# Two up tiles at a time by seven block products, and the norm's row scale at the end of the ConvFFN

## The chip, the cores and the metric

One Trainium2 chip, one of its cores. The metric is the device time in microseconds from launch to end. The engines are TensorE (matmuls into PSUM), VectorE, ScalarE, GpSimd and SyncE; each runs its own queue in order and waits on semaphores. SyncE and GpSimd issue nearly all DMAs here. In the profile they are PE, DVE, ACT, POOL and SP.

## The reference

One inference step of a decoder trunk: 512 prompt rows and 8 sample rows, 520 columns here since activations are kept with features on partitions. D_MODEL = 1024, two layers. Layer 0 mixes by a short gated convolution, layer 1 by dilated attention in three groups; each is followed by a ConvFFN with D_FF = 2816:

```
def rmsnorm(x, g):
    r = lax.rsqrt(jnp.mean(xf * xf, axis=-1, keepdims=True) + EPS)
    return (xf * r).astype(x.dtype) * g

def convffn(h, hist, w_gate, w_up, conv_w, conv_b, w_down):
    gconv, new_hist = causal_dwconv(h @ w_gate, hist, conv_w)     # 3 taps along the sequence
    return (jax.nn.silu(gconv + conv_b) * (h @ w_up)) @ w_down, new_hist

hp = rmsnorm(xp, norm_ffn[i])
fp, fh_p = convffn(hp, ...)
xp = xp + fp
```

Everything is float32. The last rows of h @ w_gate are outputs too.

## The kernel before

**Products.** A float32 operand is split in two parts for the float32r matmul: a high part (a rounding copy, ScalarE) and a low part (operand less high part, VectorE). Of a product the terms high x high, high x low and low x high are made. The weights stream from HBM in chunks of 1024 rows x 128 columns (512 KB) into four slots `wraw`; ScalarE makes `wh`, VectorE `wl`, two buffers each. A chunk is prepared when the chunk two before it has been used (`step` and `splits`). SyncE loads the chunk four ahead when a slot's low part is made (`load`, L464).

**A chunk on TensorE** (`wide_products`, L2016 to L2020) is eight k-steps. Each has five matmuls: one of 512 columns that streams high and low part of half the activations beside each other, and four of 256 or 264. `products` (L1998) makes the same in six matmuls. The three terms stream 3 x 520 = 1560 columns a k-step in both.

**ConvFFN.** Gate and up: 22 tiles of 128 features in 11 bodies of four chunks (gate, up, gate, up), into the PSUM banks `acc[:, 0]` and `acc[:, 1]`. In layer 1 the first body's second pair goes to `M` and `N`, since it begins while the attention's output is still being added. The norm's weight is on the activations ahead of the product; its row scale r is known only a chunk or more after the stage has begun, so it is applied at the read-outs: `wide_gate_out` multiplies a gate by r (ScalarE first copies the low x wide part, `keep_low`), then come the convolution (`conv_act` on ScalarE, `taps` on VectorE), silu (L1028), silu x r (`gate_rows`, L1572), and the product with the up tile (`product_out`), whose high and low part (`y_hi`, `y_lo`) are made at once. Down: eight tiles, each from three chunks that cover the 22 k-steps, then `residual` adds the tile to x.

**Entering a stage.** `rms` on ScalarE copies the high part of the square sum, takes what work is due (`early`), then waits for TensorE's mean square and makes r with Ln and Exp; the table for silu is loaded after it. `rms` on VectorE makes the low part of the square sum, does its own early split and waits for r.

**Order.** All orders are written out by hand, engine by engine. The bodies are hardware loops (`Fori`) on each engine, with semaphore targets worked out in registers. GpSimd copies the KV caches from HBM to HBM in pieces that wait for counts of used chunks.

## Time and profile before

| | |
|---|---|
| runs | 1195.51, 1195.6, 1196.05 us; median 1195.6 us |
| profiled execution | span 1194.2 us from first to last instruction |
| granted TensorE clock, mean | 1.000 |
| instructions | 26318, of these 10352 matmuls |
| VectorE, ScalarE busy | 774.9 us, 546.5 us |
| DMA | 193.19 MB, 162 GB/s mean |

The page gives no time of the profiled execution outside its span; its span is 1.4 us under the median of the runs. Times below are microseconds from the span's start. In an order of time a row is one instruction, or several merged (x2), with start and duration; listed durations of neighbours overlap on an engine, so the pace is the distance of the starts. Gate/up of layer 0 runs from about 186 to 420 us, that of layer 1 from about 834 to 1072.

### The profile page before, as it was taken

The page shows a single profiled execution, that of the slowest core. Times are in us where ns is not written, and L with a number is a line of the kernel's source. Part 1 is how long each engine was busy: PE and PEld are TensorE (multiplying, and loading weights), DVE is VectorE, ACT ScalarE, POOL GpSimd, SP SyncE. Part 2 cuts the span into 40 slices and gives each one's busy share as a digit, 9 for nine tenths or more (in the row PEclk, how much of TensorE's full clock was granted, in tenths as well). Part 3 has the DMA queues.
Part 4 walks back from the last instruction along what each step waited for, and adds up shares of the span by engine and source line. Part 5 has one row for each costly group of instructions (what it writes and reads, how often), then busy time and mean ns, then how long its engine had stood idle before and what let it go on. Part 6 is the DMA issues. An engine that isn't in the chain of part 4 may idle for free.

```text
span 1194.2 us, 26318 instructions
## 1 busy us (share of the span) xinstructions
PE 1188.3 (100%) x10352; PEld 1139.5 (95%) x10352; DVE 774.9 (65%) x1425; ACT 546.5 (46%) x956; POOL 21.1 (2%) x50
## 2 busy tenths in 40 slices
PE   9999999999999999999999999999999999999999
PEld 8999999999999999999999999988999999999998
DVE  6766677766777644445686776868887776774333
ACT  6333345444444532225466565556654454442221
POOL 0000000000000000000000000000000000000000
PEclk9999999999999999999999999999999999999999
DMA  8454535565454555455567766669545454546542
GB/s 222 127 164 150 177 110 172 172 191 160 145 152 136 169 159 155 143 174 170 157 204 195 221 176 192 194 159 238 151 147 153 137 173 154 151 146 183 133 115 44
DMA packets 285909, 193.19 MB, mean 162 GB/s; under 512 B 40433, under 2 KB 282153, under 8 KB 284678
## 3 DMA queue, kind: packets, MB, share of 16 engines
q1 hardware_dynamic: 282636, 137.04, 42.2%
q0 software_dynamic: 1792, 54.43, 12.8%
q8 instruction: 57, 0.93, 0.4%
q10 hardware_dynamic: 1402, 0.61, 0.2%
q14 instruction: 22, 0.18, 0.0%
HBM read 184.52 MB, written 64.16 MB: 208 GB/s over the span
## 4 chain that ended last, share of the span: by engine, by line
PE 93%; DVE 4%; ACT 1%; DMA 1%; issue 1%; SPq 0%; DVEq 0%; POOL 0%; ACTq 0%; POOLq 0%
PE acc L2016 22%; PE acc L1998 15%; PE acc L2020 12%; PE acc L2017 11%; PE acc L2018 11%; PE acc L2019 11%; PE acc L2054 3%; PE N L1985 1%; PE M L2054 1%; PE N L2309 1%; DVE wl L1294 1%; PE acc L2289 1%; PE M L1985 1%; DVE u L1795 1%; PE M L2258 1%
## 5 line engine op out<-in xcount | busy, mean ns | idle before, releaser
L886 ACT ACTIVATE wh<-wraw 128x1024 fp32r<-128x1024 f32 (+1 forms) x211 | 218.0, 1033 | 276.4 <-PE acc L2020 176.4
L1294 DVE TENSOR_TENSOR wl<-wraw,wh 128x1024 fp32r<-128x1024 f32 (+1 forms) x211 | 252.8, 1198 | 130.3 <-ACT wh L886 102.5
L2016 PE MATMUL acc<-h_both,wh 128*128 128x512 f32 x832 | 315.6, 379 | 0.0
L2020 PE MATMUL acc<-h_both,wl 128*128 128x264 f32 x832 | 231.3, 278 | 0.0
L2017 PE MATMUL acc<-h_both,wh 128*128 128x264 f32 x832 | 229.6, 276 | 0.0
L2018 PE MATMUL acc<-h_both,wh 128*128 128x264 f32 x832 | 229.6, 276 | 0.0
L2019 PE MATMUL acc<-h_both,wl 128*128 128x256 f32 x832 | 226.8, 273 | 0.0
L1998 PE MATMUL acc<-h_both,wh 128*128 128x256 f32 (+2 forms) x1152 | 178.2, 277 | 0.4 <-DVEq L1709 0.2
L2018 PEld LDWEIGHTS acc<-h_both,wh 128*128 128x128 f32 x832 | 157.2, 189 | 22.2
L2016 PEld LDWEIGHTS acc<-h_both,wh 128*128 128x128 f32 x832 | 159.7, 192 | 0.1
L2017 PEld LDWEIGHTS acc<-h_both,wh 128*128 128x128 f32 x832 | 157.2, 189 | 0.0
L2019 PEld LDWEIGHTS acc<-h_both,wl 128*128 128x128 f32 x832 | 157.2, 189 | 0.0
L2020 PEld LDWEIGHTS acc<-h_both,wl 128*128 128x128 f32 x832 | 157.2, 189 | 0.0
L1998 PEld LDWEIGHTS acc<-h_both,wh 128*128 128x128 f32 x1152 | 152.0, 190 | 1.9 <-DVEq L1729 1.0
L2016 PE MATMUL acc<-y_both,wh 128*128 128x512 f32 x378 | 143.5, 380 | 0.0
L1998 PE MATMUL acc<-h_both,wl 128*128 128x256 f32 (+1 forms) x576 | 111.5, 275 | 0.0
L2020 PE MATMUL acc<-y_both,wl 128*128 128x264 f32 x378 | 105.1, 278 | 0.0
L2018 PE MATMUL acc<-y_both,wh 128*128 128x264 f32 x378 | 104.3, 276 | 0.0
L2017 PE MATMUL acc<-y_both,wh 128*128 128x264 f32 x378 | 104.3, 276 | 0.0
L2019 PE MATMUL acc<-y_both,wl 128*128 128x256 f32 x378 | 103.0, 273 | 0.0
L1998 PEld LDWEIGHTS acc<-h_both,wl 128*128 128x128 f32 x576 | 87.5, 190 | 0.0
L2018 PEld LDWEIGHTS acc<-y_both,wh 128*128 128x128 f32 x378 | 71.4, 189 | 10.1
(289 smaller groups left out, 1726.6 us busy)
## 6 DMA issues: line engine op xcount, KB each, us to landing
out_dram<-in_cache_kv_d_dram POOLq DMA_DIRECT2D x24, 1364.0 KB, 6.4
wraw<-in_ffn_w_gate_dram SPq DMA_DIRECT2D x44, 512.0 KB, 3.9
wraw<-in_ffn_w_up_dram SPq DMA_DIRECT2D x44, 512.0 KB, 3.9
wraw<-in_attn_w_qkv_dram SPq DMA_DIRECT2D x36, 512.0 KB, 4.2
out_dram<-in_cache_kv_d_dram POOLq DMA_DIRECT2D x8, 2044.0 KB, 8.3
wraw<-in_ffn_w_down_dram SPq DMA_DIRECT2D x32, 448.0 KB, 3.8
wraw<-in_sc_w_in_dram SPq DMA_DIRECT2D x23, 512.0 KB, 4.0
wraw<-in_ffn_w_down_dram SPq DMA_DIRECT2D x16, 512.0 KB, 4.2
```

The lines of the kernel that those rows point to most:

```text
L886: nc.scalar.activation(wh[c % 2][:, 0:k], wraw[:, c % 4, 0:k], ACT.Copy).then_inc(hi_done, 1)
L1294: V.tensor_tensor(wl[c % 2][:, 0:k], wraw[:, c % 4, 0:k], wh[c % 2][:, 0:k].bitcast(F32), ALU.subtract).then_inc(split_done, 1)
L1795: ch.after(V.tensor_reduce(out=sums, in_=k, axis=AX_X, op=ALU.add))
L1985: return T.transpose(out, in_, ident[0:k, 0:k])
L1998: ins = T.matmul(pair_bank(dst, b, cut), w[c % 2][:, k, :], paired(a[:, k0 + k], b, cut), start=(first and k == 0 and n == 0), stop=(last ...
L2016: T.matmul(wide, h[:, k, :], wide_pairs(both[:, :, k0 + k]), start=start, stop=False)
L2017: T.matmul(rest, h[:, k, :], paired(high, 1, CUT), start=start, stop=False)
L2018: T.matmul(rest, h[:, k, :], paired(low, 1, CUT), start=False, stop=False)
L2019: T.matmul(some, l[:, k, :], paired(high, 0, CUT), start=False, stop=stop)
L2020: ins = T.matmul(rest, l[:, k, :], paired(high, 1, CUT), start=False, stop=stop)
L2054: ins = T.matmul(pair_bank(dst, b, cut), w[c % 2][:, k, :], paired(a[:, k], b, cut), start=(first and n == 0), stop=(last and n == 2))
L2258: T.matmul(M[QB * t:QB * t + QB, h2, 0:2 * P], k[s, 0, q0:q0 + QB], k[s, 1, k0:k0 + 2 * P], start=True, stop=True)
```

## The change

In bodies 1 to 8 of the 11, in both layers, the two gate chunks stay as they are and the two up tiles are made together. The 256 x 1024 block of weights and the 1024 x 520 activations are each seen as 2 x 2 blocks: the two tiles by the two halves of the rows (512 each), and the activations' row halves by two column sets of 260. Seven products of blocks take the place of eight, with sums of blocks ahead (Strassen's scheme in Winograd's form) and sums of products behind. Each block product is four k-steps of three matmuls of 260 columns, 12 matmuls into one bank.

- Weight side, each body: four sums of 128 x 512 on VectorE (`s1`, `s2`, `s3`, and one in place in `wraw`). A body has six units to split, the last half as large, instead of four chunks; three buffers take turns. Slots 2 and 3 are loaded when the body's fifth unit is split.
- Activation side, once a layer: eight copies of x times the norm's weight (`gain_x`, ScalarE, placed between the square sum's high part and Ln), four sums of 1040 elements (`part_sums`, VectorE), their high parts (`sums_high`) and low parts (`sums_low`). Two of the sums stand ahead of the first product.
- Behind the products: four copies of block results out of PSUM (`keep_part`, ScalarE) and three folds (VectorE) a body. Three blocks are added onto what is in a bank.
- The row scale r is no more in the up read-out (`gate_rows` goes); silu writes into `yf`, and down's read-out multiplies by r (`scaled_residual`).
- The splits of y move: `y_high` and `y_low` of tiles 0 to 6 stand one a body in bodies 2 to 8, the others in bodies 9, 10 and after.
- The last down tile of layer 0 is made by `products`. The loops of the ConvFFN and of the cache copies are written out, with their waits renumbered.

Cut to its core:

```diff
+                    for s in range(4):
+                        if it == 0:
+                            sp.wait_ge(split_done, gu.chunk(0, s) + 1)
+                        elif it - 1 in PAIRED and s >= 2:
+                            sp.wait_ge(split_done, gu.chunk(it - 1, 4) + 5)
+                        else:
+                            sp.wait_ge(split_done, gu.chunk(it - 1, s) + 5)
+                        w, i = ((wg, wg, wu, wu)[s], s % 2) if it in PAIRED else ((wg, wu)[s % 2], s // 2)
+                        sp.dma_start(wraw[:, s], w[:, :, (2 * it + i) * P:(2 * it + i + 1) * P]) \
+                            .then_inc(chunk_loaded[s], 16)
...
+            def gain_x(norm, ks):
+
+                for k in ks:
+                    nc.scalar.activation(gained_x[:, k], x[:, k], ACT.Copy,
+                                         scale=params[:, GAIN[norm] + k:GAIN[norm] + k + 1]).then_inc(gx_ready, 1)
+
...
+                def unit_hi(it, c, used):
+
+                    act.wait_ge(chunk_used, used + 1)
+                    j = 3 * paired_done(layer, it)
+                    if c in (0, 1, 2):
+                        act.wait_ge(chunk_loaded[c], gu.loads(it, c))
+                    else:
+                        act.wait_ge(sums_ready, j + (1, 3, 2)[c - 3])
+                    hi, raw = ring_hi(c), ring_raw(c)
+                    n = KH if c == 5 else DK
+                    nc.scalar.activation(hi[:, 0:n], raw[:, 0:n], ACT.Copy).then_inc(hi_done, 1)
+
+                def keep_part(dst, bank):
+                    nc.scalar.activation(dst, bank[:, 0:HALF], ACT.Copy).then_inc(snap, 1)
...
+                def paired_gates(it):
+
+                    f, j = 2 * it, 3 * paired_done(layer, it)
+                    if it - 1 in PAIRED:
+                        unit_hi(it, 1, gu.chunk(it - 1, 4))
+                        unit_hi(it, 2, gu.chunk(it - 1, 5))
+                    else:
+                        unit_hi(it, 2, gu.chunk(it - 1, 3))
+                    keep_gate(it, 0, 0, acc[:, 0])
+                    unit_hi(it, 3, gu.chunk(it, 0))
+                    conv(f)
+                    silu(f)
+                    keep_gate(it, 1, 1, acc[:, 1])
+                    unit_hi(it, 4, gu.chunk(it, 1))
+                    act.wait_ge(part_done, j + 1)
+                    act.wait_ge(y_ready, f + y0)
+                    keep_part(C1[:, 0], M[:, 0])
+                    conv(f + 1)
+                    unit_hi(it, 5, gu.chunk(it, 2))
+                    act.wait_ge(part_done, j + 2)
+                    keep_part(C2[:, 1], N[:, 0])
+                    for g in SPLIT_AT.get(it, ()):
+                        y_high(g)
+                    act.wait_ge(chunk_used, gu.chunk(it, 3) + 1)
+                    keep_part(C1[:, 1], M[:, 0])
+                    unit_hi(it + 1, 0, gu.chunk(it, 3))
+                    silu(f + 1)
+                    act.wait_ge(part_done, j + 3)
+                    keep_part(C2[:, 0], N[:, 1])
+
+                def gates(it):
+                    if it - 1 in PAIRED:
+                        unit_hi(it, 1, gu.chunk(it - 1, 4))
                     for i in range(2):
...
+            def part_sums(layer, which):
+
+                b = (slice(0, ALL_CUT), slice(ALL_CUT, HALF))
+                h1, h2 = gained_x[:, 0:KH], gained_x[:, KH:DK]
+                t12, t34 = raw_sums[:, 0], raw_sums[:, 1]
+                for i in which:
+                    dve.wait_ge(gx_ready, DK * layer + (KH if i == 0 else DK))
+                    dst, a, c = ((t12[:, :, :, b[0]], h1[:, :, :, b[1]], h1[:, :, :, b[0]]),
+                                 (t12[:, :, :, b[1]], h2[:, :, :, b[1]], t12[:, :, :, b[0]]),
+                                 (t34[:, :, :, b[0]], h2[:, :, :, b[1]], h1[:, :, :, b[1]]),
+                                 (t34[:, :, :, b[1]], h2[:, :, :, b[0]], t12[:, :, :, b[1]]))[i]
+                    if i == 3:
+                        dve.wait_ge(t_sum, 4 * layer + 3)
+                    V.tensor_tensor(dst, a, c, ALU.subtract).then_inc(t_sum, 1)
+
...
+            def sums_low(layer):
+
+                for n in range(4):
+                    j, i = n // 2, n % 2
+                    dve.wait_ge(t_hi, 4 * layer + n + 1)
+                    b = slice(i * ALL_CUT, (i + 1) * ALL_CUT)
+                    V.tensor_tensor(h_sums[:, 1, j, :, :, b], raw_sums[:, j, :, :, b],
+                                    h_sums[:, 0, j, :, :, b].bitcast(F32), ALU.subtract).then_inc(t_lo, 1)
...
+                    gate_out(0, acc[:, 0])
+                    conv(0)
+                    splits(gu, 0, 2)
+                    part_sums(layer, (1, 3))
+                    dve.wait_ge(chunk_used, gu.chunk(0, 1) + 1)
+                    product_out(0, acc[:, 1])
+                    dve.wait_ge(chunk_used, gu.chunk(0, 2) + 1)
+                    gate_out(1, M)
+                    splits(gu, 0, 3)
+                    conv(1)
+                    dve.wait_ge(chunk_used, gu.chunk(0, 3) + 1)
+                    product_out(1, N)
+                    sums_low(layer)
...
+                def first_gates():
+
+                    n = body_kept(layer, 0)
+                    dve.wait_ge(chunk_used, gu.chunk(0, 0) + 1)
+                    wide_gate_out(0, acc[:, 0], n + 1)
+                    conv(0)
+                    splits(gu, 0, 1)
+                    part_sums(layer, (1, 3))
+                    dve.wait_ge(chunk_used, gu.chunk(0, 1) + 1)
+                    wide_product_out(0, acc[:, 1], n + 2)
+                    dve.wait_ge(chunk_used, gu.chunk(0, 2) + 1)
+                    wide_gate_out(1, acc[:, 0], n + 3)
+                    splits(gu, 0, 2)
+                    conv(1)
+                    dve.wait_ge(chunk_used, gu.chunk(0, 3) + 1)
...
+                def lower_product(it):
+
+                    f, j = 2 * it + 1, 4 * paired_done(layer, it)
+                    dve.wait_ge(snap, j + 4)
+                    dve.wait_ge(chunk_used, gu.chunk(it, 5) + 1)
+                    ch.after(V.tensor_tensor(C2, C2, M[:, 0:1, 0:HALF].to_broadcast([P, 2, HALF]), ALU.add))
+                    dve.sem_inc(acc_free, 2)
+                    silu_kept(f)
+                    V.tensor_tensor(cut2(yf[:, f]), sum_view(C2), cut2(yf[:, f]), ALU.mult).then_inc(y_ready, 1)
+
+                def paired_gates(it):
+
+                    f, n, i = 2 * it, body_kept(layer, it), paired_done(layer, it)
+                    a11, a12 = wraw[:, 2, 0:KH], wraw[:, 2, KH:DK]
+                    a21, a22 = wraw[:, 3, 0:KH], wraw[:, 3, KH:DK]
+                    s1, s2, s3 = s12[:, 0:KH], s12[:, KH:DK], ring_raw(5)
+                    if it - 1 in PAIRED:
+                        unit_lo(it, 1)
+                        lower_product(it - 1)
+                    unit_lo(it, 2)
+                    dve.wait_ge(chunk_loaded[3], gu.loads(it, 3))
+                    ch.after(V.tensor_tensor(s1, a21, a22, ALU.add))
+                    V.tensor_tensor(s2, s1, a11, ALU.subtract).then_inc(sums_ready, 1)
+                    if it == 1:
+                        dve.wait_ge(out_done, 16 * (2 if layer == 0 else 7 + 2 * NG))
+                    V.tensor_tensor(s3, a11, a21, ALU.subtract).then_inc(sums_ready, 1)
+                    dve.wait_ge(chunk_used, gu.chunk(it, 0) + 1)
+                    wide_gate_out(f, acc[:, 0], n + 1)
+                    unit_lo(it, 3)
+                    dve.wait_ge(sums_ready, 3 * i + 2)
+                    V.tensor_tensor(a21, a12, s2, ALU.subtract).then_inc(sums_ready, 1)
+                    conv(f)
+                    dve.wait_ge(chunk_used, gu.chunk(it, 1) + 1)
+                    wide_gate_out(f + 1, acc[:, 1], n + 2)
+                    unit_lo(it, 4)
+                    dve.wait_ge(snap, 4 * i + 1)
+                    dve.wait_ge(chunk_used, gu.chunk(it, 2) + 1)
+                    V.tensor_tensor(C1[:, 0], M[:, 1, 0:HALF], C1[:, 0], ALU.add)
+                    conv(f + 1)
+                    unit_lo(it, 5)
+                    for g in SPLIT_AT.get(it, ()):
+                        y_low(g)
+                    unit_lo(it + 1, 0)
+                    dve.wait_ge(snap, 4 * i + 3)
+                    dve.wait_ge(chunk_used, gu.chunk(it, 4) + 1)
+                    ch.after(V.tensor_tensor(C1[:, 1], N[:, 0, 0:HALF], C1[:, 1], ALU.add))
+                    silu_kept(f)
+                    V.tensor_tensor(cut2(yf[:, f]), sum_view(C1), cut2(yf[:, f]), ALU.mult).then_inc(y_ready, 1)
+
+                def gates(it):
+                    n = body_kept(layer, it)
...
+                def scaled_residual(it, c, par, m, n, wide):
+
+                    xm = x[:, m]
+                    dve.wait_ge(chunk_used, dn.chunk(it, c) + 1)
+                    if wide:
+                        V.tensor_tensor(wide_set(t1), wide_part(acc[:, par], 1), wide_set(r), ALU.mult)
+                        V.tensor_tensor(rest_set(t1), rest_part(acc[:, par]), rest_set(r), ALU.mult)
+                        ch.after(V.tensor_tensor(wide_set(y32), wide_part(acc[:, par], 0), wide_set(r), ALU.mult))
+                        dve.sem_inc(acc_free, 1)
+                        ch.after(V.tensor_tensor(xm, t1[:], xm, ALU.add))
+                        V.tensor_tensor(wide_set(xm), wide_set(y32), wide_set(xm), ALU.add).then_inc(x_ready, 1)
+                    else:
+                        ch.after(V.tensor_tensor(cut2(t1[:]), by_half(acc[:, par]), cut2(r[:]), ALU.mult))
+                        dve.sem_inc(acc_free, 1)
+                        V.tensor_tensor(xm, t1[:], xm, ALU.add).then_inc(x_ready, 1)
+                    dve.wait_ge(x_ready, n + 1)
 
                 def down(it, last):
...
+                def block_product(bank, c, k0, both, x0, b, onto=False):
+
+                    h, l = ring_hi(c), ring_lo(c)
+                    for k in range(KH):
+                        for n, (w, i) in enumerate(((h, 0), (h, 1), (l, 0))):
+                            ins = T.matmul(bank[:, 0:HALF].rearrange("p (n h) -> p n h", h=2), w[:, k0 + k, :],
+                                           paired(both[:, i, x0 + k], b, ALL_CUT),
+                                           start=(not onto and k == 0 and n == 0), stop=(k == KH - 1 and n == 2),
+                                           skip_group_check=onto)
+                    return ins
+
+                def paired_ups(it):
+
+                    i = paired_done(layer, it)
+                    a, b_, d, e = M[:, 0], M[:, 1], N[:, 0], N[:, 1]
+                    t12, t34 = h_sums[:, :, 0], h_sums[:, :, 1]
+
+                    def split(c):
+                        pe.wait_ge(split_done, gu.chunk(it, c) + 5)
+
+                    pe.wait_ge(acc_free, gu.tile(it, 0) + 2)
+                    split(2)
+                    block_product(a, 2, 0, h_both, 0, 0).then_inc(part_done, 1)
+                    block_product(b_, 2, KH, h_both, KH, 0).then_inc(chunk_used, 1)
+                    split(3)
+                    pe.wait_ge(t_lo, 4 * layer + 4)
+                    block_product(d, 3, 0, t12, 0, 0).then_inc(part_done, 1)
+                    pe.wait_ge(snap, 4 * i + 1)
+                    block_product(a, 3, KH, t12, 0, 1, True).then_inc(chunk_used, 1)
+                    split(4)
+                    block_product(e, 4, KH, t34, 0, 1).then_inc(part_done, 1)
+                    pe.wait_ge(snap, 4 * i + 2)
+                    block_product(d, 4, 0, h_both, KH, 1, True).then_inc(chunk_used, 1)
+                    split(5)
+                    pe.wait_ge(snap, 4 * i + 3)
+                    block_product(a, 5, 0, t34, 0, 0, True).then_inc(chunk_used, 1)
+
                 if norm is not None:
...
-            rms(1, lambda: splits(S_GU0, 0, 0))
+            rms(1, lambda: (part_sums(0, (0, 2)), splits(S_GU0, 0, 0)))
...
-            rms(3, lambda: splits(S_GU1, 0, 1))
+            rms(3, lambda: (splits(S_GU1, 0, 1), part_sums(1, (0, 2))))
...
+                    ch.after(V.tensor_tensor(tm, down, r[:, :, lo:hi], ALU.mult))
```

## Rows read from the trace of the kernel before

**Rows 1.** The page: engines' busy time, and the chain by engine.

```profile
PE 1188.3 (100%) x10352; PEld 1139.5 (95%) x10352; DVE 774.9 (65%) x1425; ACT 546.5 (46%) x956; POOL 21.1 (2%) x50
...
PE 93%; DVE 4%; ACT 1%; DMA 1%; issue 1%; SPq 0%; DVEq 0%; POOL 0%; ACTq 0%; POOLq 0%
```

**Rows 2.** Order of time, TensorE, gate/up of layer 0: start, duration (us), line, operation.

```profile
400.38 0.38 PE L2016 MATMUL acc<-h_both,wh 128*128 128x512 f32 x1
...
409.69 0.38 PE L2016 MATMUL acc<-h_both,wh 128*128 128x512 f32 x1
```

**Rows 3.** Order of time, TensorE, the last down tile of layer 1.

```profile
1186.09 0.28 PE L2578 MATMUL acc<-y_both,wl 128*128 128x264 f32 x1
...
1189.12 0.28 PE L2578 MATMUL acc<-y_both,wl 128*128 128x256 f32 x1
```

**Rows 4.** Order of time, ScalarE, entry into gate/up of layer 0.

```profile
187.13 0.73 ACT L908 ACTIVATE h_both<-x,params 128x520 fp32r<-128x520 f32 x1
187.77 0.62 ACT L912 ACTIVATE sv<-x 128x520 f32<-128x520 f32 x1
189.78 0.64 ACT L919 ACTIVATE y_both<-ssq 128x520 fp32r<-128x520 f32 x1 [1.39 <-DVE ssq L1313]
191.38 0.38 ACT L900 ACTIVATE u<-acc 128x256 f32<-128x256 f32 x1 [0.96 <-PE acc L2020]
191.66 1.05 ACT L886 ACTIVATE wh<-wraw 128x1024 fp32r<-128x1024 f32 x1
192.61 0.69 ACT L924 ACTIVATE r<-N,small 128x520 f32<-128x520 f32 x1
193.32 0.64 ACT L926 ACTIVATE r<-r 128x520 f32<-128x520 f32 x1
193.98 1.28 ACT L1102 ACT_TABLE_LOAD   x1
195.27 0.24 ACT L932 ACTIVATE u<-hist_ffn 128x16 f32<-128x16 f32 x1
195.80 0.83 ACT L940 ACTIVATE cv<-u,params 128x536 f32<-128x536 f32 x1 [0.29 <-DVE u L1566]
```

**Rows 5.** Order of time, VectorE, the same entry.

```profile
194.55 0.42 DVE L1561 TENSOR_TENSOR u<-acc,u 128x256 f32<-128x256 f32 x1
...
195.29 0.41 DVE L1566 TENSOR_TENSOR u<-u,r 128x256 f32<-128x256 f32 x1
196.67 0.78 DVE L1353 SCALAR_TENSOR_TENSOR cv<-u,params,cv 128x536 f32<-128x536 f32 x1 [0.96 <-ACT cv L940]
197.48 0.78 DVE L1355 SCALAR_TENSOR_TENSOR cv<-u,params,cv 128x536 f32<-128x536 f32 x1
198.18 1.23 DVE L1294 TENSOR_TENSOR wl<-wraw,wh 128x1024 fp32r<-128x1024 f32 x1
199.33 0.68 DVE L1572 TENSOR_TENSOR t<-sv,r 128x512 f32<-128x512 f32 x1
```

**Rows 6.** The page: DMA issues, KB each, median us to landing.

```profile
wraw<-in_ffn_w_up_dram SPq DMA_DIRECT2D x44, 512.0 KB, 3.9
```

**Rows 7.** Order of time, TensorE: third chunk of layer 0, first of layer 1's second body.

```profile
196.89 0.38 PE L2016 MATMUL acc<-h_both,wh 128*128 128x512 f32 x1
...
859.72 0.38 PE L2016 MATMUL acc<-h_both,wh 128*128 128x512 f32 x1
```

**Rows 8.** Order of time, ScalarE, entry into gate/up of layer 1.

```profile
852.51 0.69 ACT L924 ACTIVATE r<-N,small 128x520 f32<-128x520 f32 x1 [1.81 <-PE N L2034]
853.24 0.64 ACT L926 ACTIVATE r<-r 128x520 f32<-128x520 f32 x1
```

**Rows 9.** TensorE's first matmuls; then windows: stretch, busy (count) by engine, PEclk, DMA.

```profile
1.26 4.20 PE L2062 MATMUL acc<-rms_ones 128*128 128x128 f32 x18 [1.26 <-POOL rms_ones L745]
...
10.68 1.09 PE L1985 MATMUL M<-ident,big 128*128 128x128 f32 x8
...
1193.00:1193.50 0.50, 0.00 (x0) 0.00 (x0) 0.00 (x0) 0.00 (x0) 0.00 (x0) 0.67 0.47 136
```

346 lines of the change are left out of this document (222 added, 124 removed).

## The prediction

> **What bounds the kernel now.** The page's first section comes first, then its chain: TensorE is busy for 1188.3 of 1194.2 us and carries 93% of the chain [rows 1]. I then read TensorE's order of time inside a gate/up stage. The wide matmul of one k-step starts at 400.38 and that of the 14th after it at 409.69, so 0.665 us a k-step, in which five matmuls stream 1560 columns without a hole [rows 2]. Elsewhere, too, matmuls start on the previous one's heels. So a gate/up chunk (eight k-steps) costs 5.32 us and only two things move the time: fewer columns on TensorE, and pauses it does not have now. Whether pauses come is read from ScalarE and VectorE around the two entries into gate/up, since VectorE has just 65% load on average and gains most of the new work.
>
> **1. TensorE in a paired body.** The two up tiles cost 16 k-steps x 0.665 = 10.64 us. Their seven block products are 7 x 4 x 3 = 84 matmuls of 260 columns, each block into one PSUM bank. Nearest row: the end of the last down tile, also three products a k-step into one bank, with 264 and 256 columns. From 1186.09 to 1189.12 it makes nine triples, 3.03 us / 27 = 0.112 us a matmul [rows 3]. 84 x 0.112 = 9.41 us, 1.23 us less a body, **19.7 us over 16 bodies**. Bounds: by columns alone (0.665 x 260/1560 = 0.111) 21 us; at 0.116, an estimate from the steps between single matmuls, 14 us. I take 0.112. The Trainium skill's page "TensorE: Matmul & The Clock Gate", section "Back-to-back issue gap", gives columns divided by 2.4 GHz plus 2.5 ns, 110.8 ns here; by that rule the term would be 21.3 us. The triples of rows 3 are slower, and the sum goes by them.
>
> **2. Steady paired body (20.05 us: 10.64 + 9.41).** Costs from start to start, when nothing is waited for [rows 4, 5]: on VectorE 1.15 for 1024 elements, 0.61 for 512 or 520 (the listed time less 0.08, as 198.18 + 1.23 against 199.33), 0.34 for 256; a gate read-out 1.15 (194.55 to the end of the operation at 195.29) and 0.15 to release the bank, an estimate; the two taps 0.81 + 0.70. Per body VectorE then has five and a half low splits 6.36, four tile sums 2.55 (one waits for its forerunner), two gate read-outs 2.6, two taps pairs 3.02, three folds of block products 1.6, two products 1.2, one low part of y 0.6: 18.0 us. One hole can't be filled: the second gate's read-out waits for ScalarE's copy, which stands behind the first tile's silu, 1.2 us. 19.1 against 20.05, so VectorE holds the pace with 0.9 us a body. The deadlines hold too: with time counted from the body's start, the split of the next body's first gate is done at 18.8 (needed 20.05), those of units 3, 4, 5 at 8.5, 14.2, 16.6 (needed 13.3, 16.0, 18.7). ScalarE has about 11 us of work. The loads are the same four of 512 KB, now with slots 2 and 3 asked for together at 14.2; one lands in 3.9 us [rows 6], and the pair, even one after the other, by 22, where the split that needs it has until 30.7. Cost zero, cover 0.9 us a body.
>
> **3. Entry, layer 0: moved work.** After the copy of the square sum (189.78 to 190.33) ScalarE now makes eight scaled copies of x, 0.64 apart (187.13 to 187.77), to 195.5; only then come the gate's low copy 0.28, the split of the third chunk 0.95, Ln 0.71, Exp 0.64 and the table load 1.29 [rows 4]. So r is ready at 198.0 instead of 193.96, the table at 199.3. Tile 0's gate is read out from 198.07, its bank is free at 199.3, and the third chunk started at 196.89 before [rows 7]: **pause 2.4**. Then the convolution's ScalarE part (0.25 + 0.83) ends at 200.4, the taps take 1.5, the fourth chunk's split 1.15, and ahead of tile 0's product stand two of the activation sums, 1040 elements each, 2.4. The product (0.34 + 0.34 + 0.41 and the release) frees its bank at 206.65. TensorE is there at 199.3 + 5.32 = 204.6: **pause 2.05**. The fourth chunk ends at 212.0.
>
> **4. First paired body, layer 0.** From 212.6 VectorE has one unbroken queue: product 1.2, split 1.15, four low parts of the activation sums 4.6, split 1.15, three tile sums 1.9, gate read-out 1.3, split 1.15, tile sum 0.6, taps 1.5, the hole of 1.2, read-out 1.3, split 1.2: 230.9. TensorE needs ScalarE's copy of the first block product at 212.0 + 10.64 + 2.69 + 1.34 = 226.65. ScalarE makes it behind the second gate's copy, which stands behind that silu, and it is done at 229.6: **pause 3.0**, at whose end the split is nearly ready too. Later bodies start with VectorE 0.9 us a body to the good.
>
> **5. Layer 1.** ScalarE had waited 1.81 us ahead of Ln (852.51) [rows 8], so of the 5.1 us of scaled copies 3.2 come through: r at 857.1, table at 858.4. The read-out, convolution part, taps and split of the next body's first gate end at 862.25; TensorE is free at 859.72 [rows 7]: **pause 2.55**. VectorE goes on without rest: two activation sums 2.4, product 0.8, read-out 0.9, split 1.15, taps 1.5, 0.9 for silu, product 0.8, four low parts 4.6, then the split of unit 2, done at 876.65. TensorE is there at 862.25 + 10.64: **pause 3.75**. Three tile sums, read-out, split: 881.0 against 876.65 + 2.69: **pause 1.65**. Tile sum, taps, silu, copy: 885.45 against 882.35: **pause 3.1**.
>
> **6. Small ones.** The last tile's two halves get one more product each; the second, 256 elements at 0.41 and its wait, is on the end's path: 0.45. The narrow last down tile of layer 0 has six matmuls for five a k-step: 0.15. Layer 0's residuals grow by 0.4 each, one under 14 us of TensorE; the last has 0.5 us of room ahead of the mean square (my reading of VectorE's order of time there); without it 0.4. Written-out loops: TensorE shows no hole at a body's turn, so nothing is gained there; what it could cost is instruction fetches, and as the attention part runs written out today with TensorE busy all through, I take 0 and keep 2 us, an estimate, in the range. The cache copies wait for the same work.
>
> **Sum.** Pauses 7.4 + 11.05 = 18.5; -19.7 + 18.5 + 0.6 = -0.6 on the span of 1194.2: 1193.6. The median of the runs is 1195.6, 1.4 above that profile's span, so **1195.0** if the clock holds. The queues above are sums of rows in order; 3% on VectorE's durations moves the pauses by 1.4 us, and an operation dropped or late by 1 us in sections 4 or 5 moves them by 1.
>
> **The clock.** In this trace the granted clock is 1.00 through every pause, but none is above 0.6 us. The first 18 matmuls, of 128 columns, take 4.20 us where eight later ones take 1.09, which is half speed, and at the end the granted clock is 0.67 on average in the half microsecond from 1193.00, 1.4 us after the last matmul [rows 9]. So a pause of 3 us may bring the 1.2 GHz level. I price a fall at 2 us, 4 us at half speed as at the start. Where VectorE's next deadline binds anyway it is absorbed: the first in layer 0 by the second pause, the early ones of layer 1 by the later. Only the last pause of each entry is unprotected. The same page's section "Why this matters for your kernels" warns against idle gaps between bursts of matmuls; by that rule the time is that of rival (a). The trace bears it out only at its two ends.
>
> **Forecast (0.30):** the entries give the whole gain back and the clock holds: **1195.0**, its own range 1192 to 1198 (bounds of the block matmul and of VectorE's durations together).
>
> **Rivals.**
> (a) The same, and the clock falls at the last pause of one entry or of both (0.28): 1197 to 1199.
> (b) Faster (0.24). The first paired body's pauses (3.0 in layer 0, 3.75 + 1.65 + 3.1 in layer 1) stay away because VectorE's queue comes through sooner than I lay it out, while those of body 0 stay (they hang on r, which is plain). For it: waits on loop registers go with constants. Against: my durations are of rows that wait on constants already. 1195.0 - 11.5 = 1183.5; with half of it 1189.
> (c) Slower (0.13): VectorE becomes the engine that sets the steady pace. Its margin is 0.9 in 19.1, so this decides from 5% more a body. At 8% it is 0.6 us a body, 14 bodies: +8; at 12%, +20: 1203 to 1215. Place: the wait ahead of each body's block products. For it: the folds read PSUM through broadcast and interleaved views that no row shows. Against: today's read-outs are interleaved too and cost what plain operations do.
> (d) Slower (0.05): a matmul that adds to a bank whose group was closed and read costs more than its neighbours; at 0.116 on all 84, 16 x 84 x 0.004 = 5.4: 1200.4.
> That the change does not do what it says is out: the 84 half-width matmuls for 80 are in the code, with nothing that could merge or skip them.
>
> **How the numbers follow.** A measurement of this kernel can tell about 0.2%, 2.4 us, so 1193.2 and 1198.0 are the borders. Faster: (b) 0.24 and 0.05 of the forecast, 0.29. Same: 0.25 of the forecast and 0.14 of (a), 0.39. Slower: the other 0.14 of (a), (c) 0.13, (d) 0.05, 0.32. The range of 8 in 10 leaves out the low half of (b) and most of (c): 1186 to 1202.
>
> **What would show it.** Block matmuls 0.112 apart; 20.05 us from one paired body to the next with no pause in bodies 2 to 8; pauses of 2.4 and 2.05 in body 0 of layer 0 and 2.55 at the start of body 1 in layer 1; in body 1 pauses of 3.0 and 8.5; r at 198.0 and 857.1; PEclk 1.00 throughout, or below it after those pauses alone (a). Wrong if body 1 runs through (b), or if bodies 2 to 8 show pauses (c).

## The result, and the profile after

Four runs of the changed kernel took 1200.64 to 1206.24 us, median 1203.7, against 1195.51 to 1196.4 of the kernel before on the same chip (median 1195.8): ratio 1.0065, 95% interval [1.0053, 1.0078]. So the change costs 8 us; 1195.0 with a range of 1186 to 1202 had been forecast. The profiled run took 1202.2 us, of which the trace spans 1200.1, 6.0 more than before. The page of the kernel after, busy time, chain and the DMA issues, to be read against [rows 1, 6]:

```profile
PE 1178.3 (98%) x10438; PEld 1134.4 (95%) x10438; DVE 850.4 (71%) x1462; ACT 594.8 (50%) x1088; POOL 21.2 (2%) x50
...
PE 80%; DVE 11%; ACT 4%; DMA 2%; issue 2%; ACTq 0%; SPq 0%; DVEq 0%
...
wraw<-in_ffn_w_up_dram SPq DMA_DIRECT2D x44, 512.0 KB, 5.2
```

TensorE is busy for 10 us less, though the ledger below has 20 us less in the paired bodies: part of the difference is four stretches of 3.41 us at half clock (below), in which the same work takes 6.8 us more. Its share of the chain falls from 93% to 80%; VectorE's rises from 4% to 11%. Work was saved, and pauses took its place. A steady paired body is what it was meant to be. TensorE's order of time in layer 0: the first matmul of one body, the first block product (with the last gate matmul before it), and the first matmul of the next:

```profile
319.94 0.38 PE L2338 MATMUL acc<-h_both,wh 128*128 128x512 f32 x1
...
330.46 0.28 PE L2342 MATMUL acc<-h_both,wl 128*128 128x264 f32 x1
330.58 0.50 PE L2521 MATMUL M<-h_both,ring 128*128 128x260 f32 x3
...
339.96 0.38 PE L2338 MATMUL acc<-h_both,wh 128*128 128x512 f32 x1
```

10.64 us of gates and 9.38 us for 84 block products, 0.1117 us each, which answers to the 0.112 of [rows 3]: 20.02 us, 1.26 less than the 21.28 of before. The waits of TensorE over the whole kernel, grouped (total us, times, longest) say where it stood instead:

```profile
PE M L2521 <- ACT sv L1187: 8.0, 4, 2.8
PE M L2521 <- DVE ring L1859: 2.7, 1, 2.7
PE acc L2338 <- DVEq L1790: 2.1, 1, 2.1
PE N L2376 <- ACT r L1021: 1.9, 1, 1.9
...
PE acc L2338 <- DVE wl L1492: 0.8, 1, 0.8
```

A wait's time is that of TensorE's idle stretch. A pause below is the step between two matmul starts less the usual 0.11 us, which is some 0.15 us more than the idle stretch. From the last matmuls of bodies, stages and tiles I made this ledger of the two traces (us, after less before; predicted in brackets):

- 16 paired bodies: -20.2 (-19.7)
- layer 0, body 0: +4.5 (+4.45); body 1: +4.95 (+3.0)
- layer 1, bodies 0 and 1: +3.84 and +7.70, together +11.5 (+11.05, otherwise placed)
- layer 0, bodies 4 and 5: +2.6 (0); layer 1, bodies 6 and 7: +1.1 (0)
- layer 1's down stage: +1.05 (0); narrow tile and tail: +0.2 and +0.46 (+0.15 and +0.45)
- all other stages together: -0.2. Sum +6.0.

### The profile page after: what moved, and what is told of

The parts are those of the page before. It is cut to its first block, busy times and chain, and to the rows that moved or that the text cites. A ratio compares the mean times of both kernels' runs of the same rounds, so it can differ in the third digit from the quotient of the medians.

```text
span 1200.1 us, 25294 instructions
## 1 busy us (share of the span) xinstructions
PE 1178.3 (98%) x10438; PEld 1134.4 (95%) x10438; DVE 850.4 (71%) x1462; ACT 594.8 (50%) x1088; POOL 21.2 (2%) x50
## 4 chain that ended last, share of the span: by engine, by line
PE 80%; DVE 11%; ACT 4%; DMA 2%; issue 2%; ACTq 0%; SPq 0%; DVEq 0%
PE acc L2320 17%; PE acc L2338 15%; PE acc L2342 8%; PE acc L2339 8%; PE acc L2340 8%; PE acc L2341 7%; PE M L2521 5%; PE N L2521 4%; PE acc L2376 2%; DMA wraw<-in_ffn_w_up_dram 2%; DVE wl L1492 1%; PE N L2307 1%; DVE wl L1859 1%; ACT big L1053 1%; DVE h_sums L1561 1%
## 5 line engine op out<-in xcount | busy, mean ns | idle before, releaser
L983 ACT ACTIVATE wh<-wraw 128x1024 fp32r<-128x1024 f32 (+1 forms) x147 | 150.8, 1026 | 267.2 <-PE acc L2342 156.5
L1492 DVE TENSOR_TENSOR wl<-wraw,wh 128x1024 fp32r<-128x1024 f32 (+1 forms) x147 | 174.4, 1186 | 90.3 <-ACT wh L983 82.8
L2338 PE MATMUL acc<-h_both,wh 128*128 128x512 f32 x576 | 219.4, 381 | 2.3 <-DVEq L1790 2.1
L2342 PE MATMUL acc<-h_both,wl 128*128 128x264 f32 x576 | 160.6, 279 | 0.0
L2340 PE MATMUL acc<-h_both,wh 128*128 128x264 f32 x576 | 159.4, 277 | 0.0
L2339 PE MATMUL acc<-h_both,wh 128*128 128x264 f32 x576 | 159.4, 277 | 0.0
L2341 PE MATMUL acc<-h_both,wl 128*128 128x256 f32 x576 | 157.5, 273 | 0.0
L2320 PEld LDWEIGHTS acc<-h_both,wh 128*128 128x128 f32 x1152 | 152.1, 190 | 1.6 <-DVEq L2051 1.0
L2338 PE MATMUL acc<-y_both,wh 128*128 128x512 f32 x356 | 135.3, 380 | 0.8 <-DVE wl L1492 0.8
L2340 PEld LDWEIGHTS acc<-h_both,wh 128*128 128x128 f32 x576 | 109.3, 190 | 15.6
L2338 PEld LDWEIGHTS acc<-h_both,wh 128*128 128x128 f32 x576 | 110.9, 193 | 3.1 <-DVEq L1790 2.3
L2341 PEld LDWEIGHTS acc<-h_both,wl 128*128 128x128 f32 x576 | 109.3, 190 | 0.0
L2342 PEld LDWEIGHTS acc<-h_both,wl 128*128 128x128 f32 x576 | 109.3, 190 | 0.0
L2339 PEld LDWEIGHTS acc<-h_both,wh 128*128 128x128 f32 x576 | 109.2, 190 | 0.0
L2339 PE MATMUL acc<-y_both,wh 128*128 128x264 f32 x356 | 98.3, 276 | 0.0
L2340 PE MATMUL acc<-y_both,wh 128*128 128x264 f32 x356 | 98.3, 276 | 0.0
L2320 PEld LDWEIGHTS acc<-h_both,wl 128*128 128x128 f32 x576 | 87.5, 190 | 0.0
```

Source lines behind the costliest of these rows:

```text
L983: nc.scalar.activation(wh[c % 2][:, 0:k], wraw[:, c % 4, 0:k], ACT.Copy).then_inc(hi_done, 1)
L1492: V.tensor_tensor(wl[c % 2][:, 0:k], wraw[:, c % 4, 0:k], wh[c % 2][:, 0:k].bitcast(F32), ALU.subtract).then_inc(split_done, 1)
L2320: ins = T.matmul(pair_bank(dst, b, cut), w[c % 2][:, k, :], paired(a[:, k0 + k], b, cut), start=(first and k == 0 and n == 0), stop=(last ...
L2338: T.matmul(wide, h[:, k, :], wide_pairs(both[:, :, k0 + k]), start=start, stop=False)
L2339: T.matmul(rest, h[:, k, :], paired(high, 1, CUT), start=start, stop=False)
L2340: T.matmul(rest, h[:, k, :], paired(low, 1, CUT), start=False, stop=False)
```

## The experiments

Each ratio is against runs of the kernel before on the same chip. Times of the changed kernel's own runs spread over 5.6 us, so effects below some 3 us are read from the traces, body by body.

**Pairs from body 2 on.**

```
-PAIRED = tuple(range(1, 9))
+PAIRED = tuple(range(2, 9))
-                        for g in SPLIT_N[it][i]:
+                        for g in SPLIT_N.get(it, ((), ()))[i]:
-                    if it == 1:
+                    if it == PAIRED[0]:
```

> Bodies 2 to 8 of each layer are paired, body 1 goes back to four plain chunks; gains, sums of h, narrow part and written-out loops stay. Theory (the work of the entry into a layer's gate/up stage, the sums of h and the gains, stands in the queues of VectorE and ScalarE when the first paired body needs them): body 1 takes 21.3 us again in both layers instead of 24.97 and 27.72, body 2 stays at 20.0 because VectorE has caught up during the plain body, so 3.7 + 6.4 = 10.1 us less than with eight pairs, about 1193.6 us. The rise of body 0 (4.5 us in layer 0, 3.8 at chunk 3 of layer 1) stays. Rival (a first paired body is slow by its own handshake between snapshots and block products, whatever stands before it): the 3.7 and 6.4 us move to body 2, and with two pairs fewer the time is 1204 to 1206 us.

1196.99 us, ratio 1.0013 [1.0003, 1.0022]. Layer 0: body 1 at 21.28, body 2 at 20.02, as the theory says. In both layers the first paired body, body 2, takes 20.02, which speaks against the rival. But in layer 1 body 1 takes 27.14 us without a pair in it, where 21.3 were expected: a pause of 4.2 us, and 3.41 us at a granted clock of 0.50 from its end on. TensorE there, then VectorE just before:

```profile
875.50 0.77 PE L2338 MATMUL acc<-h_both,wh 128*128 128x512 f32 x1 [4.02 <-DVE wl L1492]
```
```profile
868.21 4.70 DVE L1561 TENSOR_TENSOR h_sums<-big,h_sums 128x1040 fp32r<-128x1040 f32 x4 [0.24 <-ACT h_sums L1060]
872.83 0.42 DVE L1783 TENSOR_TENSOR u<-acc,u 128x256 f32<-128x256 f32 x1
```

The four low parts of the sums stand for 4.7 us ahead of an ordinary gate read-out. So the cause is the queue behind r, not the pair. In the trace 5.5 of the 10.1 us came: 5.8 are missing here, and the late pairs (below) happened to cost 1.5 less than in the changed kernel's trace.

**No pairs at all.**

```
-PAIRED = tuple(range(1, 9))
+PAIRED = ()
-                gain_x(1, range(DK))
-            rms(3, lambda: gain_x(3, range(DK)))
+            rms(3)
```
(and no sums_high, part_sums and sums_low anywhere; the high and low parts of y are made one a tile from body 1 on)

> No body is paired and no gains and sums of h are made; the row scale at the down read-out, the narrow part there and the written-out loops stay. Theory: they cost only what the tail of the last body grew by, 0.46 us, so 1196.0 to 1196.8 us, with every body at 21.28 us. Rival (writing the loops out, or the scale at the read-out, costs something in each body or tile that the trace puts elsewhere): 1198 us or more, with bodies over 21.3 us or down tiles over their lengths in the kernel before.

1196.48 us, ratio 1.0007 [0.9998, 1.0016]; span 1194.2, as before, and every body but the first at 21.28. Loops written out and the moved row scale cost nothing that can be seen inside the span. Outside it they may: from the span to the time it is 2.06 to 2.12 us in all eleven runs, against 1.51 to 1.62 in the 28 of the kernel before. The same 2.0 to 2.2 stand in every run of the changed kernel and of the other experiments, so some 0.5 us comes with what they all share; which part of it is not shown.

**Cache copies elsewhere.**

```
     def place(self, old):
         it, c = divmod(old, 4)
-        return self.chunk(it, c + (1 if c == 3 and it in PAIRED else 0))
+        return self.chunk(it + 1, 0) if c and it in PAIRED else self.chunk(it, c)
```

> Only the places of the cache copies change: a copy that fell at the end of a paired body waits for the first gate chunk of the body after it, so that it is no longer issued less than 1 us before the pair of weight tiles. Theory (the 2 MB copy delays the weight pair from 5 to 11.2 us, and ScalarE then waits 5.8 us for it): no body over 20.3 us among bodies 2 to 8 of layers 0 and 1, no pause at their starts, so 2.6 + 1.1 = 3.7 us less, about 1200.0 us. Rival (the late pair is only late by the order of loads on its own queue, and TensorE's pause there is VectorE's backlog): the pauses stay where they are, and the time stays at 1201 to 1206 us.

1199.03 us, ratio 1.0027 [1.0018, 1.0036]. Bodies 2 to 8 are at 20.02 in both layers: the 3.7 us are gone. First the changed kernel: GpSimd's issue, the pair on SyncE's queue, ScalarE's wait for it and TensorE's pause (orders of time), and the DMA view of 268 to 286 us (queue, packets, MB, then issues, KB each, us to landing):

```profile
271.05 0.49 POOL L824 DMA_DIRECT2D out_dram<-in_cache_kv_d_dram  x1 [22.21 <-PE M L2521]
...
271.73 7.20 SPq L567 DMA_DIRECT2D wraw<-in_ffn_w_up_dram  x2
...
283.02 1.06 ACT L1184 ACTIVATE ring<-wraw 128x1024 fp32r<-128x1024 f32 x1 [5.81 <-DMA wraw<-in_ffn_w_up_dram]
...
294.13 0.38 PE L2521 MATMUL M<-h_sums,wh 128*128 128x260 f32 x1 [2.01 <-ACT sv L1187]
```
```profile
q1 hardware_dynamic: 3884, 1.96, 40.4%
q0 software_dynamic: 48, 2.09, 36.2%
...
out_dram<-in_cache_kv_d_dram POOLq DMA_DIRECT2D x1, 2044.0 KB, 9.0
wraw<-in_ffn_w_up_dram SPq DMA_DIRECT2D x2, 512.0 KB, 11.9
```

The same stretch with the copies moved, the pair and then ScalarE's copy of it:

```profile
wraw<-in_ffn_w_up_dram SPq DMA_DIRECT2D x2, 512.0 KB, 4.6
```
```profile
277.10 1.06 ACT L1184 ACTIVATE ring<-wraw 128x1024 fp32r<-128x1024 f32 x1 [0.28 <-PE M L2521]
```

A pair issued 0.7 us behind a copy of 2 MB lands in 11.9 us, one without a copy in 4.6. The copy's data went in 32 packets of 65 KB (the other 16 are of 4 bytes), two for each of the 16 DMA engines, the weights' in packets of 0.5 KB. The DMA view of 272 to 278 us of the changed kernel has the copy's queue alone (a packet counts whole where it starts, so the share is over 100%):

```profile
q0 software_dynamic: 32, 2.09, 108.5%
```

The first packets of the pair start at 278.5 us. The Trainium skill's page "DMA: Bandwidth & Descriptors", section "Queues, rings and completion order", says that each DMA engine takes turns between its queues packet by packet. The trace bears out that a long turn of the copy comes first. It does not show a turn between the copy's two packets on an engine (the second ones start at 275.6 to 276.7), so both would have to be one turn; why the pair waits for the whole copy is not shown. SyncE was held too: its two issues take 7.20 us (the row above), 0.99 with the copies moved.

**VectorE's copy of the rows first.**

```
-                for f in range(SPLIT_N[FK // 2 - 1][1][-1] + 1, FK):
-                    y_low(f)
                 if layer == 0:
                     dve.wait_ge(y_ready, y0 + FK)
                     ch.after(V.memset(ssq[:], 0.0))
                 rows_flush(rows_n)
+                for f in range(SPLIT_N[FK // 2 - 1][1][-1] + 1, FK):
+                    y_low(f)
```

> On VectorE the copy of the state rows stands ahead of the last four remainders of y instead of behind them. Theory (ScalarE's five issues of row DMAs wait for that copy and stand ahead of the first split of the last down stage): the pause of 0.96 us at the entry of layer 1's down stage goes, the split of its first tile is made some 5 us earlier, and the last matmul ends 1.0 us earlier for the same time of entry: about 1202.7 us. Rival (the pause belongs to the last remainders of y themselves, which TensorE needs first): it stays or grows to 1.5 us, since the remainders come later, and the time is 1203.7 to 1204.5 us.

1200.57 us, ratio 1.0035 [1.0022, 1.0047]. The down stage of layer 1, up to its last tile, takes 112.93 us against the changed kernel's 113.99, as the kernel before (112.94): the pause is gone. VectorE's order of time at that entry, the changed kernel and then the experiment:

```profile
1080.72 2.52 DVE L1814 TENSOR_TENSOR y_both<-big,y_both 128x520 fp32r<-128x520 f32 x4
1083.17 0.68 DVE L1721 COPY newh_tok<-N 99x512 f32<-99x512 f32 x1
1087.10 1.23 DVE L1492 TENSOR_TENSOR wl<-wraw,wh 128x1024 fp32r<-128x1024 f32 x1 [3.25 <-ACT wh L983]
```
```profile
1081.86 0.68 DVE L1721 COPY newh_tok<-N 99x512 f32<-99x512 f32 x1
1082.46 2.52 DVE L1814 TENSOR_TENSOR y_both<-big,y_both 128x520 fp32r<-128x520 f32 x4
1085.88 1.23 DVE L1492 TENSOR_TENSOR wl<-wraw,wh 128x1024 fp32r<-128x1024 f32 x1 [0.89 <-ACT wh L983]
```

This stage starts 1.1 us later in the experiment, so its split is 2.4 us earlier, not the 5 expected, and that is enough. The median is 3.1 us under the changed kernel's, of which this explains 1.05; the rest lies within the spread of the changed kernel's runs. The two traces span the same (1200.2 and 1200.1 us), since in the experiment's the clock fell behind the second pause of layer 0's body 0, which takes 27.92 us there instead of 26.25:

```profile
207.32:210.73 3.41, 3.41 (x15) 3.15 (x15) 3.15 (x6) 2.85 (x5) 0.00 (x0) 0.50 0.33 98
```

**r ahead of the gains** (on top of pairs from body 2 on).

```
     def first_gate():
-        act.wait_ge(vec_out, 48)
-        gain_x(1, range(DK))
...
-            rms(3, lambda: gain_x(3, range(DK)))
+            rms(3, lambda: gain_x(3, range(2)))
...
                     conv(0)
+                    act.wait_ge(vec_out, 48)
+                    gain_x(norm, range(0, 1))
                     step(gu, 0, 1)
                     silu(0)
+                    gain_x(norm, range(1, 3))
...
                     conv(1)
+                    part_sums(layer, (0,))
```

> As the kernel with pairs from body 2 on, and the gains and the sums of h are moved behind the row scale r: no gain stands before the read-out of the first gate tile of layer 0, and only two of the eight in front of r in layer 1; the other gains stand in pieces of one to three in ScalarE's body 0, the four sums and their splits in pieces of one in VectorE's bodies 0 and 1. Nothing is left out. Theory (what costs at the entries is the order of the two queues there, r behind eight gains of 0.62 us above all): body 0 of layer 0 takes 21.7 us instead of 26.25, bodies 0 and 1 of layer 1 take 29.4 + 21.3 = 50.7 us instead of 60.4, together 14.2 us less than with pairs from body 2 on, about 1182.8 us. Rival (the sums cost what they are long, some 10 us of VectorE and 9 of ScalarE, and come back as pauses wherever they stand): pauses of 3 us or more in body 1 or 2 of each layer, 1188 to 1195 us.

1185.8 us, ratio 0.9914 [0.99, 0.9928], a gain of 9.8 us. ScalarE's Ln in layer 1, changed kernel and experiment:

```profile
857.64 0.69 ACT L1021 ACTIVATE r<-N,small 128x520 f32<-128x520 f32 x1
```
```profile
845.83 0.69 ACT L1021 ACTIVATE r<-N,small 128x520 f32<-128x520 f32 x1 [0.57 <-PE N L2364]
```

Counted from the last chunk of the attention's output stage that is 25.5 and 22.3 us; before, 22.3 too. Body 0 is back at 21.73 and 29.41 us. The edit moves the gains and the sums together, so the 8.4 us of body 0 (both layers) are not divided between the two; layer 1's body 1 went from 27.14 to 22.12 us with the four low parts away from its read-out. Of the 14.2 us expected 10.8 came in the trace: pauses of 0.9 us are left in body 2 of each layer and 0.8 in layer 1's body 1. The rival's 3 us and more did not come.

**Everything together.** In one kernel: pairs from body 2 on, r ahead of the gains, the cache copies elsewhere, VectorE's copy of the rows first.

> As the one before, and with the cache copies away from the weight pairs and VectorE's copy of the rows ahead of its last four remainders. Theory (the four causes are separate and add up): the late pairs' 2.2 us and the 1.0 us at layer 1's down stage go too: 1182.8 - 3.2 = 1179.6 us, with bodies 2 to 8 all at 20.0 us. Rival (with TensorE earlier, another load or the key and value output DMAs come late in their place): the same 1182 to 1184 us, with pauses elsewhere in bodies 2 to 8.

1182.58 us (1182.3 to 1183.58), ratio 0.9888 [0.9873, 0.9904]: 13.1 us faster than the kernel before, 21 than the change as made. Against the experiment before it the late pairs and the down stage's pause give 3.35 us of span, where 3.2 were expected. The time is not the 1179.6 of the theory, which counted from 1182.8 for the experiment before it (1185.8 measured); it is in the rival's 1182 to 1184, but not for the rival's reason: bodies 4 to 8 are at 20.02 in both layers, and the pauses left in bodies 1 and 2 stood in the experiment before it too. TensorE's waits, grouped:

```profile
PE M L2529 <- ACT sv L1188: 1.4, 2, 0.7
...
PE acc L2346 <- DVE wl L1494: 0.6, 1, 0.6
```

**Needless products in a pause** (on the changed kernel).

```
+                def idle_products(bank, count):
+
+                    for n in range(count):
+                        T.matmul(bank[:, 0:HALF].rearrange("p (n h) -> p n h", h=2), rms_ones_r,
+                                 paired(h_both[:, 0, n % DK], 0, ALL_CUT), start=True, stop=True)
+
...
                     pe.wait_ge(acc_free, gu.tile(it, 0) + 2)
+                    if it == 1 and layer:
+                        idle_products(e, 24)
...
+                    if it == 1:
+                        idle_products(e, 26)
                     pe.wait_ge(snap, 4 * i + 1)
```

> All eight pairs as in the change. In body 1 TensorE makes 26 needless products of 260 columns into a free bank (2.9 us) before the block product that waits for the first snapshot, in both layers, and 24 (2.7 us) before the first block product of layer 1; nothing else differs. Theory (each pause of 2 us or more there is followed by a stretch at a granted clock of 0.5, and the slow matmuls behind it cost 1.7 us where no later wait takes them up): the clock stays at 1.0 behind 230 us, body 1 of layer 0 takes 23.2 us instead of 24.97, body 1 of layer 1 stays at 27.7 us, since VectorE's work sets both waits there; 1.7 us less in the trace. Rival (the low clock has nothing to do with the pause, or costs nothing): the stretch at 0.5 is there as before and body 1 stays at 25.0 us. The times of the runs of the change spread over 5 us, so the trace decides.

1201.0 us, ratio 1.004 [1.0025, 1.0054]. The granted clock is the column of 1.00 or 0.50 behind the engines' busy time. First the changed kernel, its pause in body 1 of layer 0 and three low stretches, then the experiment over the filled pauses:

```profile
227.00:230.00 3.00, 0.38 (x4) 0.19 (x2) 1.79 (x6) 2.15 (x6) 0.00 (x0) 1.00 0.00 0
231.19:234.60 3.41, 3.41 (x18) 3.41 (x18) 3.38 (x6) 2.84 (x8) 0.00 (x0) 0.50 0.47 141
859.24:862.65 3.41, 3.41 (x18) 3.41 (x18) 1.78 (x4) 3.28 (x6) 0.00 (x0) 0.50 0.00 0
879.72:883.13 3.41, 3.41 (x18) 3.41 (x18) 3.26 (x7) 2.22 (x5) 0.00 (x0) 0.50 0.00 0
```
```profile
229.00:234.00 5.00, 5.00 (x45) 4.92 (x44) 4.82 (x10) 4.86 (x13) 0.00 (x0) 1.00 0.25 69
877.00:884.00 7.00, 5.57 (x48) 5.25 (x47) 6.75 (x12) 2.22 (x5) 0.00 (x0) 1.00 0.01 2
```

Where the pauses are filled the clock stays at its upper level, 2.4 GHz. One trace would not settle that, since falls differ from run to run (below), but the mean granted clock is 0.998 or 0.999 in all five runs of the experiment, 0.991 to 0.996 in the changed kernel's four. Body 1 of layer 0 takes 23.43 us instead of 24.97, body 1 of layer 1 stays at 27.73. So the low level, 1.2 GHz for 3.41 us, costs 1.5 us here, 1.7 us in body 0 of the rows-first trace above, where no later deadline binds, and nothing where one does.

**The sums spread further** (on everything together).

```
                         if it == 1:
-                            sums_high(layer, 0, i)
-                            sums_high(layer, 1, i)
-                        silu(f)
...
+                        silu(f)
+                        if it == 1:
+                            sums_high(layer, 1, i)
...
-                    part_sums(layer, (2,))
+                    part_sums(layer, (2, 1))
```

> As the kernel with everything together (pairs in bodies 2 to 8), with the sums of h spread further: the third sum already at the end of body 0, one sum or remainder for each chunk of body 1, the high halves behind the silus instead of ahead of them. Theory (the pauses left, 0.89 us in body 2 of each layer and 0.77 us in body 1 of layer 1, are the last two remainders standing at the start of body 2 and the high halves standing ahead of the silu): bodies 2 and 3 at 20.0 us each and body 1 at 21.3 us, so 1.3 + 1.3 + 0.8 = 3.4 us less, about 1179.2 us. Rival (the first paired body has a pause of its own, whatever is ahead of it): the 0.9 us stay, about 1182 us.

1188.96 us, ratio 0.9946 [0.9932, 0.9959]: 6.4 us worse than the kernel it was to better. Body 1 takes 23.17 and 26.38 us. Body 2, the first paired one, takes 20.37 us in layer 1, against the rival, but 22.03 in layer 0, with a pause of 1.5 us, more than the 21.12 it was to better; the rival's cause is out by the experiment with pairs from body 2 on (20.02 in both layers). The other pauses are now in the plain body 1 (1.8 us in layer 0, 0.9 and 2.4 in layer 1), where a third sum stands ahead of the first read-out and another ahead of the first taps. TensorE's largest group of waits:

```profile
PE acc L2349 <- DVE wl L1497: 4.6, 3, 2.3
```

**Eight pairs with r first.**

```
-PAIRED = tuple(range(2, 9))
+PAIRED = tuple(range(1, 9))
...
+                    part_sums(layer, (3,))
+                    sums_low(layer, range(4))
```

> As the one before, but with eight pairs from body 1 on, so that gains, sums and their splits must all be made before the block products of body 1; r stays ahead of the gains. Theory (the sums are work of 10 us on VectorE, for which body 0 and a paired body 1 have no room, so order alone doesn't hide them): body 0 stays near 21.7 and 29.4 us, body 1 takes 24 to 27 us in both layers, against 21.3 us unpaired, so some 1186.6 us (1184.6 to 1190.6), worse than seven pairs. Rival (only the order was wrong: with r first all eight pairs give their 1.26 us): body 1 at 20 to 21 us, 1177 to 1179 us.

1195.89 us, ratio 0.9999 [0.999, 1.0008]. Body 0 is fine (21.83, 29.41 us), body 1 takes 28.75 and 30.25 us, more than the 24 to 27 expected. VectorE ahead of layer 1's first block product, then TensorE's groups:

```profile
867.47 1.24 DVE L1560 TENSOR_TENSOR big<-big 128x1040 f32<-128x1040 f32 x1 [0.31 <-DVE big L1804]
868.63 4.69 DVE L1568 TENSOR_TENSOR h_sums<-big,h_sums 128x1040 fp32r<-128x1040 f32 x4
873.24 1.22 DVE L1868 TENSOR_TENSOR ring<-wraw,ring 128x1024 fp32r<-128x1024 f32 x1
```
```profile
PE M L2536 <- DVE ring L1868: 6.6, 2, 5.2
PE M L2536 <- ACT sv L1192: 5.4, 2, 2.8
```

With the eighth pair body 1 is 7.5 and 9.0 us longer than a plain body. Part of that is the low clock behind the pauses (3.41 us in layer 0, 6.83 in layer 1). In neither of the two orders tried did the sums find room without a plain body between the entry and the first pair; that no order would do it is not shown.

## Why the prediction was wrong

The mechanism was right as far as it went: the entries do take the gain back. What failed is that three terms stood at zero in the sum or were left out: the late weight pairs (3.7 us), the fall of the clock (1.7) and the entry of layer 1's down stage (1.05).

- *Section 1, block matmul 0.112.* Right: 0.1117. Rival (d) is out.
- *Section 2, VectorE holds the pace.* Right. VectorE's order of time, the same fold in two bodies running, and the hole between the second gate's copy and read-out:

```profile
299.61 0.42 DVE L1907 TENSOR_TENSOR sv<-N,sv 128x260 f32<-128x260 f32 x1
...
312.13 0.42 DVE L1783 TENSOR_TENSOR u<-acc,u 128x256 f32<-128x256 f32 x1 [1.17 <-ACT u L997]
...
318.87 0.43 DVE L1907 TENSOR_TENSOR sv<-N,sv 128x260 f32<-128x260 f32 x1
```

  19.26 us while it still catches up, hole 1.17, where 19.1 and 1.2 were laid out. Rival (c) is out.
- *Section 2, "the pair, even one after the other, by 22 ... Cost zero".* **Failed; the largest miss, 3.7 us.** Two loads alone were priced at 3.9 us each [rows 6]. The copy of 2 MB that the new chunk numbers put 0.7 us ahead of them was not looked at: the section ends with the load queue and section 6 gives the copies one short sentence. Moving them removed exactly the 2.6 and 1.1 us. The price could have been read from the trace of the kernel before, where the median of 3.9 hides it: a load issued at 269.45, 2.5 us behind such a copy, took 7.8 us (its DMA view of 268 to 276 us).

```profile
wraw<-in_ffn_w_gate_dram SPq DMA_DIRECT2D x1, 512.0 KB, 7.8
```

- *Section 3, entry of layer 0, pauses 2.4 and 2.05.* Right: 2.31, and 2.01 in the two traces in which the clock held between them. r was ready at 198.07, against 198.0:

```profile
197.43 0.64 ACT L1023 ACTIVATE r<-r 128x520 f32<-128x520 f32 x1
```

- *Section 4, pause 3.0.* Right, 2.92 and 0.17 more ahead of it; the rest of the 4.95 us is the clock, to 0.2 us.
- *Section 5, layer 1, 11.05 us.* Sum right (11.5), places wrong. The sum is not luck: VectorE's queue sets where the last pause ends, wherever the earlier ones lie, and bodies 0 and 1 take 60.96 to 60.98 us in three traces with different pauses. r was ready at 859.0, which is the 857.1 foreseen, as the layer starts 2.0 us later. The fourth chunk writes into bank N, from which Ln still reads, and TensorE waits for that read: 2.10 us already in body 0, where the prediction had 2.55 at body 1's start. This wait is in the code and I had not followed it.

```profile
858.39 0.38 PE L2376 MATMUL N<-h_both,wh 128*128 128x260 f32 x1 [1.94 <-ACT r L1021]
...
879.03 0.46 PE L2521 MATMUL M<-h_both,ring 128*128 128x260 f32 x2 [2.71 <-DVE ring L1859]
...
887.67 0.49 PE L2521 MATMUL M<-h_sums,wh 128*128 128x260 f32 x2 [2.73 <-ACT sv L1187]
```

  Behind it 2.87 and 2.89 us stand for the 3.75, 1.65 and 3.1: at half speed TensorE used up the middle one. In the needless-products trace, where the clock holds there, it stands with 1.6.
- *The clock.* "If the clock holds" was the forecast; rival (a) had 0.28 and its mechanism came true, also in that a fall is absorbed where a deadline binds; its time, 1197 to 1199, did not. 2 us a fall was estimated, 1.5 to 1.7 measured, and in the profiled run only the one in body 1 of layer 0 counts. In layer 1 the fall behind the pause of 2.10 us stayed away in the trace with the copies moved, and bodies 0 and 1 take 60.98 us there against 60.96.
- *Section 6.* Tail 0.46, narrow tile 0.2, loops 0 in the span: right. **Missing: the 1.05 us at layer 1's down stage.** The four remainders of y that now stand ahead of VectorE's copy of the rows delay five DMA issues of ScalarE, and these the first split of the stage.

Together 3.7 + 1.7 + 1.05 = 6.4 of the 6.6 us between the predicted -0.6 and the measured +6.0 of span. The forecast added 1.4 us from the span to the time; for the profiled run it was 2.1, and the median run lies 1.5 us above that one. Of these 2.2 us some 0.5 is the time outside the span that every version with the loops written out has more than the kernel before. The other 1.5, from the profiled run to the median, has no shown cause. Two things point to a part each: the late pairs, since with the copies moved the runs spread over 3.3 us instead of 5.6, and over 1.3 with everything together; and the number of clock falls, since the slowest run of the changed kernel has a mean granted clock of 0.991 and the fastest 0.996.

## What to carry to other kernels

When a change makes room on the bounding engine and fills its helpers, lay out the helpers' queues at the entries of a stage, where the new one-time work meets a value that everybody waits for: here 5 us of scalings ahead of r and 10 us of sums cost as much as 16 cheaper bodies gave, and a different order with one plain body for the sums turned +8 us into -10, or -13 with the misplaced copies and the late row copy mended. A renumbering moves every DMA that is placed by these numbers; look at what each issue now stands next to. And before counting a helper's lateness, list all the waits of the bounding engine, those for a bank to be read out too.

## What the runs showed of the hardware that was not expected

- A copy of 2 MB in 32 packets of 65 KB, issued 0.7 us ahead, takes two loads of 512 KB from 4.6 to 11.9 us.
- Within 1.1 us behind four of the changed kernel's pauses of 2.1 to 2.9 us the granted clock is 0.50, each time for 3.41 us; behind the other two, of 2.18 (at 294 us) and 2.89, it stays at 1.00. In the traces with pauses of 3.75 (copies moved) and 5.40 us (eight pairs, r first) it fell inside the pause and stayed for 6.83; in the one of 4.18 (pairs from body 2 on) it fell 0.1 us before the end and stayed for 3.41. The same pause need not give the same: behind the pauses of 2.31 and 2.01 us at the entry of layer 0 the needless-products trace shows 1.00, the changed kernel's shows 0.50 behind the first, and the rows-first trace 0.50 behind the second (where nothing absorbs it: 27.92 us). The stretches of the first two, changed kernel first, and what follows for body 0: it takes 26.25 us in both, as with the fall the second pause shrinks from 2.01 to 0.34.

```profile
200.47:203.88 3.41, 3.41 (x16) 3.23 (x15) 3.32 (x4) 2.17 (x7) 0.00 (x0) 0.50 0.24 71
```
```profile
199.40:206.70 7.30, 5.51 (x40) 5.09 (x40) 6.09 (x8) 4.54 (x11) 0.00 (x0) 1.00 0.51 152
```
